# Seven column-to-row spreads moved from TensorE to transfers through DRAM, in a two-block transformer kernel

## The reference, cut to what matters

```
var = jnp.mean(o * o, axis=-1, keepdims=True)
o = o * lax.rsqrt(var + RMS_EPS) * norm_gain...
o = o.reshape(B, T, GLA_DV) * jax.nn.silu(r)
```

```
k = k.reshape(Bsz, S, B_KV_HEADS, B_HD)
k = apply_rope(rms_norm(k, knorm_g), cos, sin)
```

## Time and profile before

| what | value |
|---|---|
| median of 3 runs | 1380.01 us |
| the profiled execution | 1379.89 us, of which the span from its first to its last instruction is 1378.1 us |
| TensorE busy | 1368.8 us (99%) |
| VectorE, ScalarE, GpSimd busy | 845.5, 603.4, 179.6 us |
| TensorE's granted clock | 1.000 over the span |

### The profile page before, as it was taken

One profiled execution on the slowest core, in us unless ns is written; L12 is line 12 of the kernel. 1 busy time (PEld: TensorE's weight loads), 2 busy tenths in 40 slices (PEclk: granted clock), 3 DMA queues, 4 the chain that ended last, 5 costly groups with the idle time before them and its releaser, 6 DMA issues.

```text
span 1378.1 us, 17268 instructions
## 1 busy us (share of the span) xinstructions
PE 1368.8 (99%) x6772; PEld 1114.6 (81%) x6772; DVE 845.5 (61%) x1233; ACT 603.4 (44%) x923; POOL 179.6 (13%) x149
## 2 busy tenths in 40 slices
PE   9999999999999999999999999999999999999998
PEld 8777777778888788888888888888888888788887
DVE  6565565845443797624777456646455676877775
ACT  5354433433245454423444345434544454344551
POOL 0300010212221300000000112000001120243330
PEclk9999999999999999999999999999999999999999
DMA  6322221222352433332332324322115233222132
GB/s 213 122 77 77 78 77 62 78 77 92 92 184 77 138 107 108 107 102 82 92 107 93 111 82 146 123 77 77 62 62 170 90 116 104 91 61 63 46 138 77
DMA packets 37665, 135.49 MB, mean 98 GB/s; under 512 B 4432, under 2 KB 5456, under 8 KB 37072
## 3 DMA queue, kind: packets, MB, share of 16 engines
q1 hardware_dynamic: 37440, 134.39, 30.7%
q10 hardware_dynamic: 144, 0.00, 0.0%
HBM read 128.09 MB, written 6.29 MB: 98 GB/s over the span
## 4 chain that ended last, share of the span: by engine, by line
PE 87%; DVE 8%; issue 2%; ACT 2%; DMA 1%; POOL 0%; DVEq 0%; SPq 0%; ACTq 0%; POOLq 0%
PE ps L205 85%; PE ps L209 2%; DVE WL L152 2%; DVE TT L164 2%; DVE HL L164 1%; DMA kept<-PW 1%; DVE X L152 1%; DVE gqks L152 1%; DVE sm L170 0%; DVE KT L164 0%; DMA raw<-in_wall 0%; ACT row L202 0%; ACT HH L202 0%; DVE gE L152 0%; DVE RG L152 0%
## 5 line engine op out<-in xcount | busy, mean ns | idle before, releaser
L205 PE MATMUL ps<-HH,WH 128*128 128x512 f32 (+1 forms) x1096 | 438.2, 402 | 0.7 <-DVE HL L164 0.6
L205 PE MATMUL ps<-HL,WH 128*128 128x512 f32 (+1 forms) x1096 | 423.5, 388 | 0.0
L205 PE MATMUL ps<-HH,WL 128*128 128x512 f32 (+1 forms) x1080 | 417.8, 389 | 0.0
L152 DVE TENSOR_TENSOR WL<-raw,WH 128x1024 fp32r<-128x1024 f32 (+1 forms) x221 | 283.1, 1286 | 79.9 <-ACT WH L189 78.8
L189 ACT CAST WH<-raw 128x1024 fp32r<-128x1024 f32 (+1 forms) x222 | 231.1, 1042 | 129.0 <-PE ps L205 109.2
L205 PEld LDWEIGHTS ps<-HH,WH 128*128 128x128 f32 x1096 | 206.0, 188 | 49.1 <-issue 7.4
L205 PEld LDWEIGHTS ps<-HL,WH 128*128 128x128 f32 x1096 | 206.2, 188 | 41.5 <-issue 1.9
L205 PEld LDWEIGHTS ps<-HH,WL 128*128 128x128 f32 x1080 | 202.8, 188 | 42.8
L205 PE MATMUL ps<-PH,WH 128*128 128x512 f32 x424 | 167.5, 395 | 0.0
L205 PE MATMUL ps<-PH,WL 128*128 128x512 f32 x424 | 165.2, 390 | 0.0
L205 PE MATMUL ps<-PL,WH 128*128 128x512 f32 x424 | 165.1, 389 | 0.0
(11 more groups left out here) (224 smaller groups left out, 1448.7 us busy)
## 6 DMA issues: line engine op xcount, KB each, us to landing
raw<-in_wall SPq DMA_DIRECT2D x221, 512.0 KB, 3.6
kept<-PW SPq DMA_DIRECT2D x2, 2048.0 KB, 9.0
PWR<-kept SPq DMA_DIRECT2D x2, 2048.0 KB, 7.9
X<-in_xT SPq DMA_DIRECT2D x8, 256.0 KB, 3.7
X<-in_xT SPq DMA_DIRECT2D x4, 512.0 KB, 5.3
out_T<-X SPq DMA_DIRECT2D x7, 256.0 KB, 2.0
pe<-in_pT SPq DMA_DIRECT2D x2, 512.0 KB, 5.0
DM<-in_dm SPq DMA_DIRECT2D x1, 640.0 KB, 4.0
```

What stands on the lines that cost most here:

```text
L152: return self.put(None if self.e is None else self.e.tensor_tensor(out, x, y, op))
L205: return self.put(None if self.e is None else self.e.matmul(out, l, r, start=start, stop=stop, skip_group_check=True))
```

## The change

For all four heads of the gated attention and for key heads 1 to 3 of the last one, the row is no longer made by `pe_row` and `a_row`. The column is written to DRAM by a DMA from ScalarE's queue in pieces of one element (4 bytes): 1024 elements for a pair of gated heads (2 such writes), 512 for a key head (3 such writes). ScalarE waits for that write, then issues a DMA that reads the 2 KB row into all 128 partitions (256 KB; two for a pair of gated heads, one for a key head, 7 in all). VectorE waits for these. One pair of steps is put in between: the pair of gated heads is 20 steps, rows read at step 20 and 21 of it instead of 18 and 19 (root at 17, write at 18, read at 19), so the generator's last row is used at step 41; a key head 1 to 3 has five stages (write in 3, read in 4, VectorE's product in 5). The second gated row goes to `b_t[0]`, which is done with by then. Key head 0 stays as it was.

```diff
-                    for e_ in range(2):
-                        h = 2 * pr + e_
-                        pe_row(p, SB[2 + e_], ("gr", h), g_col(pr)[:, 4 * e_:4 * e_ + 4], ("gcol", pr))
+                    for _ in range(4):
                         yield
...
+            if h == 0:
+                pe_row(p, SB[4], ("rrow", name), col_("rope", name), ("rope col", name), [free("COL", ("rope", name))])
+            else:
+                yield
+                yield
             yield
...
-            v.wait_ge(S.act, "rope row", name)
+            if h:
+                yield
+                yield
+                v.wait_ge(S.kall, "kall", h)
+            else:
+                v.wait_ge(S.act, "rope row", name)
...
+                    yield
+                    yield
                     for e_ in range(2):
                         h = 2 * pr + e_
-                        v.wait_ge(S.act, "grow", h)
+                        v.wait_ge(S.gall, "gall", 2 * pr + 1)
                         v.wait_ge(S.pe, "go", h)
-                        v.scalar_tensor_tensor(on_t[:, h, :], ps("go", h), c("gla_norm", h), rt_("g", h), MUL,
-                                               MUL).then_inc(("on", h), free("go", h), free("RT", ("g", h)))
+                        v.scalar_tensor_tensor(on_t[:, h, :], ps("go", h), c("gla_norm", h), g_row(e_), MUL,
+                                               MUL).then_inc(("on", h), free("go", h))
...
-            a_row(a, ("rope row", name), ("rrow", name), ("rope", name))
+            if h:
+                a.wait_ge(S.dve, "rope col", name)
+                a.dma_scatter(kdram[h].rearrange("(t p) -> p t", p=P), col_("rope", name))
+                a.then_inc(("kput", h), free("COL", ("rope", name)), sig=S.kput, by=16)
+                yield
+                a.wait_ge(S.kput, "kput", h)
+                a.take("RT", ("rope", name))
+                a.dma_start(rt_("rope", name), kdram[h:h + 1, :].to_broadcast([P, T])).then_inc(("kall", h), sig=S.kall, by=16)
+                yield
+            else:
+                a_row(a, ("rope row", name), ("rrow", name), ("rope", name))
...
+                    a.wait_ge(S.dve, "gcol", pr)
+                    a.dma_scatter(gdram[pr].rearrange("e (t p) -> p (e t)", p=P), g_col(pr)).then_inc(("gput", pr), sig=S.gput, by=16)
+                    yield
+                    a.wait_ge(S.gput, "gput", pr)
                     for e_ in range(2):
                         h = 2 * pr + e_
-                        a_row(a, ("grow", h), ("gr", h), ("g", h))
+                        if pr:
+                            a.wait_ge(S.dve, "on", e_)
+                        a.dma_start(g_row(e_), gdram[pr, e_:e_ + 1, :].to_broadcast([P, T])).then_inc(("gall", h), sig=S.gall, by=16)
+                    yield
+                    for e_ in range(2):
+                        h = 2 * pr + e_
                         a.wait_ge(S.dve, "ga in", h)
                         a.copy(GH[:, h, :], RG[:, h, :]).then_inc(("ga hi", h))
                         yield
...
-                    for _ in range(5):
+                    for _ in range(7):
                         yield
...
-                g.rope(("k", h), g_rope(g, "k", h), 3)
+                g.rope(("k", h), g_rope(g, "k", h), 5 if h else 3)
```

More of the change, by code:

```diff
@@ L57 @@
              "x0", "x1", "x2", "x3", "x4", "x5", "x6", "x7", "y0", "y1", "y2", "y3", "cmask", "rope", "e0", "e1", "kept0", "kept1",
-             "again0", "again1", "out")
+             "again0", "again1", "out", "gput", "gall", "kput", "kall")
     def __init__(self, nc, ctx):
@@ L63, in __init__ @@
          self.consts, x0, x1, x2, x3, x4, x5, x6, x7, y0, y1, y2, y3, self.cmask, self.rope, e0, e1, kept0, kept1,
-         again0, again1, self.out) = self.all
+         again0, again1, self.out, self.gput, self.gall, self.kput, self.kall) = self.all
         self.raw = [raw0, raw1, raw2]
@@ L110, in wait_free @@
         if self.S.counted and name is not None:
-            found = [s for s in self.S.work if ("free", name) in s.at]
+            found = [s for s in self.S.work + [self.S.kput] if ("free", name) in s.at]
             assert found, name
@@ L212, in dma_start, with dma_scatter @@
         return self.put(None if self.e is None else self.e.dma_start(dst, src))
+    def dma_scatter(self, dst, src):
+        return self.put(None if self.e is None else self.e.dma_start(dst, src, allow_slow_non_contiguous=True))
     def prepare(self, u, last):
@@ L668, in build @@
         b_t = [at("gb0", [P, T], F32, o2 + 14336), at("gb1", [P, T], F32, ploff + 6144)]
+        gdram = nc.dram_tensor("gdram", [2, 2, T], F32, kind="Internal").ap()
+        kdram = nc.dram_tensor("kdram", [4, T], F32, kind="Internal").ap()
         S_t = at("gS", [P, 8, 256], F32, phoff)
@@ L749, in g_decays, with g_row @@
             return sz, *(x.rearrange("p (n s) -> p n s", s=2 * sz) for x in (b_t[pr], EB[lv % 2]))
+        def g_row(e_):
+            return RT[:, 0, :] if e_ == 0 else b_t[0]
         def g_col(pr):
@@ L864, in pe_rope_k @@
             yield
-            pe_row(p, SB[4], ("rrow", name), col_("rope", name), ("rope col", name), [free("COL", ("rope", name))])
+            if h == 0:
[3 more added lines that the diff above has]
+                yield
             yield
@@ L1268, in pe_program @@
                 p.tile(("k", h), H_kv)
-                p.rope(("k", h), pe_rope_k(p, h), 3)
+                p.rope(("k", h), pe_rope_k(p, h), 5 if h else 3)
             p.mark("k read")
@@ L1848, in rope_in @@
                 v.tensor_tensor(KT[:, h, :], ps(*name), RS, MUL).then_inc(("rope in", name), free(name))
-                v.rope(name, v_rope_k(v, h), 3)
+                v.rope(name, v_rope_k(v, h), 5 if h else 3)
             def query_eps():
@@ L2731, in act_program @@
                 a.tile(8)
-                a.rope(("k", h), a_rope_k(a, h), 3)
+                a.rope(("k", h), a_rope_k(a, h), 5 if h else 3)
                 a_high(a, "b", 4 + h, "norm_b", HH, S.dve, "x kv", 4 + h)
@@ L2786, in g_rope @@
             yield
+            if kind == "k" and i[0]:
+                yield
+                yield
         def pool_program(g):
```

## The result

The changed kernel takes 1416.24 us (median of 4 runs, 1415.11 to 1417.69), against 1380.28 us before in the same comparison: 1.026 of it, 95% interval 1.0244 to 1.0277. It is 36 us slower, where 1 us faster was forecast, and outside the range (1376.3 to 1385). The profiled execution took 1417.69 us with a span of 1415.9, 37.8 us more than the span of before.

A forecast was written before the change was run, and what follows sets the result against it. TensorE was taken to bound the kernel, except where VectorE sets its pace, as at the keys. Gated attention -1.2 us and keys +0.2 us made -1.0 us: 1378.9 us, range 1376.3 to 1385.

The forecast's parts named there:

- S: Time from issue of a column's write to its landing: 2.7 us at the keys, 3.0 in the gated attention.
- What is added: Prediction's part on the new transfers: write time 2.7 and 3.0 us, row read 3.5 us, issue 0.40 us.
- The third rival: First gated pair and key head 3: dear one-element pieces make VectorE wait; 1386 us at 0.08 us per piece; chance 0.25.
- its formula: Total change with p us per piece: -1.0 + 96 (p - 0.008), from 64 pieces in the gated pair and 32 at head 3.
- one wait, at head 3: Keys: 6.0 us left for write and read of 6.2, so VectorE waits 0.2 us; heads 1 and 2 have about 7.
- 5 us to spare: Second gated pair: some 5 us are over before the rows are needed, so its two rows pay in full.
- The gated attention: Its four rows by DRAM: -1.8 us of TensorE's turns, +0.6 of VectorE's delay, sum -1.2 us.
- VectorE governs at the keys: Keys: VectorE leads the clock, so TensorE's 1.3 us saved there are not got back.
- TensorE's wait for the query's square: Turn after the third query tile, at 1191 us: TensorE waits 2.2 us instead of 0.9.
- B: Time from issue of a row's read to its landing: 3.5 us, between 2.9 and 5.
- The second rival: Both places: queues have more slack, TensorE gets back all seven groups and some waits; 3.6 us, 1376.4 us; chance 0.15.
- The fourth: Writes land fast, but reads or writes fall behind a 512 KB weight transfer, losing one or two us; 1381 us; chance 0.15.

## Why the prediction was wrong

**The step that failed** is the size of S in "What is added": "The pieces are small, so I go by the 8.4 ns and by the middle of the landings: S = 2.7 and 3.0." It measured 9.4 to 10.5 us at the keys and 10.5 and 11.6 in the gated attention. The bounds of 9.0 and 14.8 nearly held it; the value chosen in them did not. S was the sum of two terms, and it was the landing (1.7 to 3.2 us, from a write of 256 KB and a load of 4 KB) that failed, not the pieces: their packets took 7.5 ns each against 8.4, but some 8.5 us passed from the last of them to the landing. So the wrong quantity was varied, and the upper bounds came near for a wrong reason (0.18 us for each piece): 1024 pieces land about 1 us later than 512, not twice as late, and 1024 of them 64 bytes apart land in 3.1 us. The rule I had quoted of the Trainium skill, "DMA: Bandwidth & Descriptors", Specifications (below 512 bytes, read-modify-write), spoke against the change and I gave it 0.25; by itself it would have misled as well, since pieces of 4 bytes far apart are below 512 bytes too and are not slow.

**The third rival** had the mechanism (VectorE's wait for the rows takes the place of TensorE's turns) and the sign, but its price was too low. With the measured S its formula gives 64 x 0.126 + 32 x 0.232 - 1.0 = 14.5 us, not 36 (per piece 0.134 and 0.24 us, less 0.008). Three things were missing. At the keys I counted one wait, at head 3; but ScalarE's wait for a write stands before the next head's root, so every head pays (roots 11.4 us apart instead of 6.5). In the second gated pair, 5 us to spare were not enough for 8.6 us more. And the lower clock after the idling adds about 9.4 us; the prediction had no term for it.

**What held.** With landings as assumed (pieces 64 bytes apart), the time is 1379.85, 0.3 us below before and 1 us above the forecast of 1378.9; the 1.56 us lost at the lower clock behind the wait at 1189.49 are more than that 1 us. The gated attention gave 1.3 us there (forecast 1.2). That VectorE governs at the keys held: TensorE's wait for the query's square grew to 2.4 us without rows and 2.5 us with them 64 bytes apart (forecast 2.2), and the time without any rows is 1.65 us below before, not 3.4. In both runs without writes or without rows at all, the keys gave 0.2 us of the gain and the gated attention the rest. It is not the whole picture: with the product moved out of the way and rows still made by TensorE nothing could be measured. The reads' B, forecast 3.5 us for one, was 3.4 to 6.0 in the change, and hidden where the writes were left out.

**The second rival**, all seven rows pay, did not come. **The fourth**, a transfer falling behind a weight transfer, was the other way round: a weight transfer issued before the pieces had landed took 9.4 to 12.1 us instead of 3.6. In the gated attention the one issued between 248 and 249 us had its first packet after 252 and landed in 11.2:

```profile
raw<-in_wall SPq DMA_DIRECT2D x1, 512.0 KB, 11.2
```

Weights are cast up to three units ahead, which hid that: ScalarE's casts waited 19.9 us in all for weights, 19.1 before.

**Open**: why close pieces land so late after their packets are done, why 8 bytes apart gives 3.3 to 7.1 us, and when the clock falls behind a wait of 2.5 us.

## What to carry to other kernels

A round trip through DRAM in small pieces has to be costed from a row of the same kind: direction, size and, above all, how close the pieces lie. Lay the data out first so that each partition writes one piece of 16 bytes or more: here that made 34 of 36 us. Then ask what stands behind the wait on the issuing engine: a wait in a queue that also does the next item's work is paid once per item. And where another engine sets the pace, as VectorE did at the keys, work taken off TensorE first lengthens TensorE's wait, and behind a longer wait the granted clock may fall: with writes that land fast the rows alone gave nothing, and 1.6 us of that were the clock. Moving VectorE's product out of the way kept the wait at 0.5 us and the clock at 1.00, and gave 2.7 us.

## What the runs showed of the hardware that was not expected

Writes of 4 bytes into 2 or 4 KB of adjacent DRAM took 9.0 to 11.5 us (512 of them) and 10.5 to 11.6 us (1024) to land, though their packets took 7.5 ns each and were done within 2 us of the issue (1024 in the first gated pair). The same writes 64 bytes apart took 1.9 to 3.9 us with packets of 7.2 ns, and the same bytes in 16-byte pieces 1.4 to 3.7. Between the last packet and the late landing no queue moved anything for 4 us. A weight transfer of 512 KB beside the slow ones took 9.4 to 12.1 us instead of 3.6. Behind a TensorE wait of 2.5 us the granted clock fell to 0.57 over 4 us in one kernel and stayed at 1.00 in another, and the fall cost 1.56 us. VectorE's product of 512 columns took 1.08 us instead of 0.69 when one operand was read with a step of 16 bytes; TensorE turned squares read with that step at hardly any cost (group after group 5.96 us apart, 5.91 without the step).
